# Twelve distances, modulo 512 bytes, between the addresses of TensorE's two operands, in a two-layer diffusion backbone

## The reference, cut to what matters

```python
for l in range(DEPTH):                      # 2
    h = _rmsnorm(x, norm_mix_pre[l]) * (1.0 + sc1) + sh1
    y, ctx_l = _mixer_context(h, *mix_w)    # or _mixer_latent: h @ w_in (1024 x 2400), attention, @ w_o (1024 x 1024)
    x = x + gt1 * _rmsnorm(y, norm_mix_post[l])
    h = _rmsnorm(x, norm_ffn_pre[l]) * (1.0 + sc2) + sh2
    x = x + gt2 * _rmsnorm(_channel_mixer(h, l, *ffn_w), norm_ffn_post[l])

def _swiglu(t, wg, wu, wd):                 # D_FF 2816 in layer 0, 3584 for each of the 8 experts
    return (jax.nn.silu(t @ wg) * (t @ wu)) @ wd
```

## Time and profile before

| | us |
|---|---|
| median of 3 runs | 1517.53 (1517.11 to 1518.0) |
| the profiled execution, own time | 1519.02 |
| its span | 1517.1 |
| TensorE busy in the span | 1472.9 (97%) |
| LDWEIGHTS busy | 1193.9 (79%) |
| VectorE busy | 1154.1 (76%) |
| ScalarE busy | 974.8 (64%) |

### The profile page before, as it was taken

One profiled execution on the slowest core, in us unless ns is written; L12 is line 12 of the kernel. 1 busy time (PEld: TensorE's weight loads), 2 busy tenths in 40 slices (PEclk: granted clock), 3 DMA queues, 4 the chain that ended last, 5 costly groups with the idle time before them and its releaser, 6 DMA issues.

```text
span 1517.1 us, 21044 instructions
## 1 busy us (share of the span) xinstructions
PE 1472.9 (97%) x7205; PEld 1193.9 (79%) x7205; DVE 1154.1 (76%) x991; ACT 974.8 (64%) x959; POOL 124.5 (8%) x180
## 2 busy tenths in 40 slices
PE   8999999999998999999999999999999999999995
PEld 4867688886876788888888888888888888888884
DVE  2676544545667479888888888888888888888885
ACT  3555633344455557777777777777777777777773
POOL 2521410000030200000000000000000000000001
PEclk9999999999999889999999999999999999999998
DMA  9976976558661979999999999999999999999991
GB/s 363 348 255 210 346 248 202 167 194 294 243 214 44 327 283 378 407 350 409 376 344 408 379 360 391 383 361 383 390 372 373 391 370 359 394 377 351 413 384 52
DMA packets 222978, 489.07 MB, mean 322 GB/s; under 512 B 9392, under 2 KB 42496, under 8 KB 222928
## 3 DMA queue, kind: packets, MB, share of 16 engines
q1 hardware_dynamic: 215376, 466.38, 83.5%
q0 software_dynamic: 7552, 22.03, 4.6%
HBM read 479.53 MB, written 8.85 MB: 322 GB/s over the span
## 4 chain that ended last, share of the span: by engine, by line
PE 92%; DVE 3%; ACT 2%; DMA 1%; issue 1%; POOL 0%; SPq 0%; POOLq 0%; DVEq 0%; ACTq 0%
PE ps L1810 24%; PE ps L1811 24%; PE ps L1815 24%; PE ps L1823 4%; PE ps L1824 3%; PE ps L1830 3%; PE ps L1861 2%; PE ps L2261 2%; PE ps L2040 1%; DMA raw<-in_w_in 1%; PE ps L1993 1%; PE ps L2015 1%; PE ps L1917 1%; PE ps L1872 1%; DVE sm L1391 0%
## 5 line engine op out<-in xcount | busy, mean ns | idle before, releaser
L1254 DVE TENSOR_TENSOR w_lo<-raw,w_hi 128x2048 fp32r<-128x2048 f32 (+1 forms) x397 | 905.2, 2285 | 177.1 <-ACT w_hi L856 176.7
L856 ACT ACTIVATE w_hi<-raw 128x2048 fp32r<-128x2048 f32 (+1 forms) x397 | 757.9, 1914 | 239.5 <-PE ps L1811 216.6
L1810 PE MATMUL ps<-w_hi,x_hi 128*128 128x512 f32 x1056 | 417.1, 395 | 1.4 <-DVE region L1481 1.4
L1811 PE MATMUL ps<-w_hi,x_lo 128*128 128x512 f32 x1056 | 411.7, 390 | 0.0
L1815 PE MATMUL ps<-w_lo,x_hi 128*128 128x512 f32 x1056 | 279.5, 390 | 0.0
L1810 PEld LDWEIGHTS ps<-w_hi,x_hi 128*128 128x128 f32 x1056 | 198.4, 188 | 42.4 <-DVE region L1481 1.8
L1815 PEld LDWEIGHTS ps<-w_lo,x_hi 128*128 128x128 f32 x1056 | 198.2, 188 | 41.9
L1811 PEld LDWEIGHTS ps<-w_hi,x_lo 128*128 128x128 f32 x1056 | 198.4, 188 | 39.8
L1810 PE MATMUL ps<-w_hi,h_hi 128*128 128x512 f32 x520 | 203.2, 391 | 4.9 <-DVE h_lo L1595 4.3
L1811 PE MATMUL ps<-w_hi,h_lo 128*128 128x512 f32 x520 | 202.4, 389 | 0.0
L1815 PE MATMUL ps<-w_lo,h_hi 128*128 128x512 f32 x520 | 137.4, 389 | 0.0
(11 more groups left out here) (274 smaller groups left out, 1101.5 us busy)
## 6 DMA issues: line engine op xcount, KB each, us to landing
raw<-in_moe_w_gate SPq DMA_DIRECT2D x112, 1024.0 KB, 6.8
raw<-in_moe_w_up SPq DMA_DIRECT2D x112, 1024.0 KB, 7.0
raw<-in_moe_w_down SPq DMA_DIRECT2D x112, 1024.0 KB, 6.8
raw<-in_w_ada SPq DMA_DIRECT2D x48, 1024.0 KB, 7.3
raw<-in_w_in SPq DMA_DIRECT2D x20, 960.0 KB, 8.4
raw<-in_ffn_w_gate SPq DMA_DIRECT2D x22, 512.0 KB, 4.6
raw<-in_ffn_w_up SPq DMA_DIRECT2D x22, 512.0 KB, 5.8
raw<-in_ffn_w_down SPq DMA_DIRECT2D x11, 1024.0 KB, 5.1
```

Of the source, the lines that this page charges most:

```text
L856: act.activation(split_hi(c, slice(0, width(c))), raw[:, r % NRAW, 0:width(c)], ACT.Copy).then_inc(hi_done, 1)
L1254: dve.tensor_sub(split_lo(c, n), raw[:, raw_of(c) % NRAW, n], split_hi(c, n)).then_inc(lo_done, 1)
L1810: pe.matmul(out, xh, split_hi(c, w), start=start, stop=False, skip_group_check=True)
L1811: last = pe.matmul(out, xl, split_hi(c, w), start=False, stop=False, skip_group_check=True)
```

## The change

It moves tensors in SBUF and nothing else. On each engine the same instructions stand in the same order, with the same shapes and the same waits; only start addresses differ.

```diff
-        w_hi = sb("w_hi", [P, NSPL - 1, UNIT], F32R)
-        w_lo = sb("w_lo", [P, NSPL - 1, UNIT], F32R)
+        w_hi = [sb("w_hi0", [P, UNIT], F32R), sb("w_hi1", [P, UNIT + 8], F32R)[:, 1:UNIT + 1]]
+        w_lo = [sb("w_lo0", [P, UNIT], F32R), sb("w_lo1", [P, UNIT + 8], F32R)[:, 4:UNIT + 4]]
+        sb("pad", [P, 512 - 16 - 256])
         qz_at = nc.sbuf_base
         qz = sb("qz", [P, 6, 2, 4, P])
-        w_hi3 = nc.alloc_sbuf_tensor_at("w_hi3", [P, UNIT], F32R, offset=qz_at)
-        w_lo3 = nc.alloc_sbuf_tensor_at("w_lo3", [P, UNIT], F32R, offset=qz_at + 4 * UNIT)
-        x_hi_at = nc.sbuf_base
-        x_hi = sb("x_hi", [P, 2, D], F32R)
-        probs_all = nc.alloc_sbuf_tensor_at("probs", [P, 2, 2, 4, 256], F32, offset=x_hi_at)
-        x_lo = sb("x_lo", [P, 2, D], F32R)
+        w_hi3 = nc.alloc_sbuf_tensor_at("w_hi3", [P, UNIT + 8], F32R, offset=qz_at - 512)[:, 2:UNIT + 2]
+        w_lo3 = nc.alloc_sbuf_tensor_at("w_lo3", [P, UNIT], F32R, offset=qz_at + 4 * UNIT - 256)
         h_hi = sb("h_hi", [P, 512], F32R)
         h_lo = sb("h_lo", [P, 512], F32R)
+        x_hi_at = nc.sbuf_base
+        x_hi = sb("x_hi", [P, 2 * D + 8], F32R)[:, 4:2 * D + 4].rearrange("p (s n) -> p s n", s=2)
+        probs_all = nc.alloc_sbuf_tensor_at("probs", [P, 2, 2, 4, 256], F32, offset=x_hi_at)
+        sb("pad_x", [P, 120])
+        x_lo = sb("x_lo", [P, 2 * D + 8], F32R)[:, 4:2 * D + 4].rearrange("p (s n) -> p s n", s=2)
+        sb("pad_x1", [P, 120])
```

More of the change, by code:

```diff
@@ L523, in split_hi @@
                 return w_hi4[:, n]
-            return w_hi[:, slot(c), n] if slot(c) < 2 else w_hi3[:, n]
+            return w_hi[slot(c)][:, n] if slot(c) < 2 else w_hi3[:, n]
         def split_lo(c, n):
@@ L528, in split_lo @@
                 return w_lo4[:, n]
-            return w_lo[:, slot(c), n] if slot(c) < 2 else w_lo3[:, n]
+            return w_lo[slot(c)][:, n] if slot(c) < 2 else w_lo3[:, n]
         block = ctx.enter_context(nc.Block())
```

## The result

The changed kernel takes 1549.18 us (median of 4 runs, 1547.66 to 1551.82) against 1517.76 us (1517.11 to 1519.02): a ratio of 1.0206, 95% interval 1.0194 to 1.0219. It is **2.1% slower**, where 1.3% faster was forecast, and lies just outside the range of 1460 to 1545 us.

What follows compares the result with a forecast made beforehand. TensorE's step between unit matmuls was taken to bound the kernel. From the profiled 1519.0 us, 16.5 (unit matmuls) and 2.9 (input projection) come off: 1499.6, forecast as 1498 us because the runs' median lies 1.5 lower; range 1460 to 1545.

Steps and rivals of the forecast that it cites:

- What bounds the kernel: TensorE, busy 97% of the span; what counts is the step between unit matmuls and their count, 5448.
- the six lines: The source lines of the unit matmuls, said to hold 83% of the span in the chain of waits.
- I take -3.3: Chosen change per 512-column unit matmul, -3.3 ns, between bounds of -13.3 and +6.3; 4968 matmuls give 16.5 us.
- the matmul step: Time from one unit matmul to the next on TensorE, 226.7 ns in the experts, forecast near 223.
- on top: Time per matmul beyond one column per cycle at 2.4 GHz: 13.3 ns over 213.3 for 512 columns.
- The second term of the sum: Input projection: 480 matmuls fall from 16.1 to 10 ns on top, a gain of 2.9 us.
- slower: the steady step is lost: Rival: switching distances keep unit matmuls from settling; 1531 us, or 1549 if each pays like a restart; chance 0.34.
- the restart: Matmuls behind an expert's transposes: seven steps of 233 ns before settling at 226.7; the worst bound, +6.3 ns.
- Off TensorE: ScalarE and VectorE splits (1914 and 2285 ns a unit) and DMAs: shifts costed at nothing, nobody waits for landings.
- No change: Rival: addresses don't matter to the unit matmul step; 1517.5 us, chance 0.15.
- much faster: Rival: all time on top of the matmuls goes, 74 us, giving 1443 us; chance of over 35 us 0.13.

Runs made afterwards that it cites:

- the run that only switches: Against the kernel before, in a new layout: distance 0 for `w_hi` and 32 for `w_lo` in all slots, switching twice within each unit; 1538.25 us.

## Why the prediction was wrong

**What bounds the kernel** was read rightly (the shares of the six lines add up to 82% as printed, not 83%), and so were the counts to within 1%. The loss stands where the argument looked for a gain: 56 blocks x 60 steps x 7.0 ns = 23.5 us, plus the longer restart units, makes the 25 to 26 us of the experts.

**The step that failed** is "I take -3.3" under the matmul step. Its reason was that the equal start is the one case in which both reads meet at each line. The runs show the reverse: where 3.3 ns less were forecast, the changed kernel has 7.0 ns more. Of eleven constant distances, 0 and 256 have the shortest step, 226.8 ns, and the others 229.0 to 237.0 (at -16 part of the stretches reach 226.7; at 4 and -4 a start off 16 bytes has its part in it). The shortest step of the input projection, 10 ns on top, which I took as a level that could be held, is one member of a sequence: before, the steps there run from 210 to 221 ns and repeat every 36 matmuls. The mean of that sequence, 16.1 on top, was the row that stood for it, as the prediction itself said and then set aside. The second term of the sum, 2.9 us gained in the input projection, rested on the same choice, and there too the step rose, from 216.1 to 218.9 ns.

**The rival "slower: the steady step is lost"** is the one that came true. It said that the distance switches every eight and four matmuls and may never settle; the run that only switches shows it, 3.3 ns on top of what its distances cost. Its upper price, each matmul paying as in the restart, 6.3 ns and 1549 us, was the result (7.0 ns in the experts, 1549.2 us). That the number agrees so closely is luck, for two parts were not priced in it: distances that are slower even when they are held, and a start off 16 bytes, which it named with the rule but left without a price; without those starts the change takes 1538.85 us. I gave it 0.34 and cut the range at 1545, below its own upper end of 1549; that cut is why the range missed.

**Off TensorE** all held. Split groups of 1914 and 2285 ns were forecast and found, so the change's shifts of 4 to 256 bytes cost ScalarE and VectorE nothing, and the longest waits in the experts of the changed kernel have none for the landing of a unit.

**No change, and much faster,** are refuted: the address distance acts, and no run has a 60-step mean under 226.7 ns. The rule of the Trainium skill cited for no change (TensorE: Matmul & The Clock Gate, "Step-by-step: what each phase is for": two independent read ports) does not describe the step of this kernel: moving the stationary operands alone by 64 bytes costs 30 us, so the measurement decides against it here. The 215.7 ns of the same page ("Wait — 56ns, not 53.3ns?") was met by no constant distance here.

**What stays open.** Why 13.3 ns are on top even at the best distance; what sets the value at each distance; and how the 20 us of the change's coarser part divide between its distances and its switching, since its 240 and 48 were not run by themselves.

## What to carry to other kernels

Where float32r matmuls and weight loads run back to back, start both operands on a multiple of 16 bytes, and keep one distance modulo 256 between moving and stationary operand for all slots; here 0 and 256 were the best of eleven. Before scattering addresses, look whether the step from matmul to matmul is one steady number: if it is, a scatter can lose it, and the one mixture that was run by itself cost more than the mean of its parts. When the only rows that show the new condition point one way, forecast that way, and let the range reach to the end of the rival that they support.

## What the runs showed of the hardware that I had not expected

- One distance with two steady steps: at -16, 226.7 ns in some stretches and 233.3 ns in others, 16 cycles of 2.4 GHz apart.
- The same at -64, with equal means: stretches whose steps are 233 or 234 ns, and stretches in which 231 and 236 ns take turns.
- Both operands starting 4 bytes past a multiple of 16: 237.0 ns a step and not 226.8, at distance 0. With the moving operand alone 237.0, with the stationary one alone 232.3.
- Settled steps by distance, 60-step means near 710 us: 0 and 256: 226.8; 64: 229.0; 16: 231.7; 508: 232.3 (start off 16 bytes); 128: 232.7 (other stretches 232.2 to 232.6); 32: 233.3; 192 and 448: 233.2; 496: 226.7 or 233.3; 4: 237.0 (start off 16 bytes).
